# Two more buffers for streamed expert weights, and a small product moved from the first eight experts to the last eight

## The reference

```python
a = rms_norm(h, g_mix)
o, sg, sh = parallel_mixers(a, ...)                # one input and one output projection
h = h + o
h = h + moe(rms_norm(h, g_ffn), w_router, b_router, w_gu, b_gu, w_dn, b_dn)
gate = sigmoid(rms_norm(h, g_ple) @ w_ple_gate)
h = h + gate * (p @ w_ple_proj)                    # p: 256 input-embedding features a token
y = rms_norm(h, g_final)
```

```python
gate, up = split(x @ w_gu[e] + b_gu[e], 2)         # w_gu[e]: 1024 x 2048
hid = (clip(up) + 1) * (min(gate, 7) * sigmoid(1.702 * gate))
y = hid @ w_dn[e] + b_dn[e]                        # w_dn[e]: 1024 x 1024
```

## Time and profile before

| | |
|---|---|
| median of 3 runs | 1286.03 us |
| profiled execution | 1286.39 us |
| its span, first to last instruction | 1284.2 us |
| TensorE busy in the span | 1216.6 us |
| bytes moved by DMA | 437.59 MB, 402.65 MB of them expert weights (384 units of 1 MB) |
| expert stage | from about 260 us to about 1231 us of the span |

### The profile page before, as it was taken

How to read it: one execution, slowest core, us unless ns; L and a number is a source line. 1 busy time by engine, 2 the same in 40 slices (tenths; PEclk the granted TensorE clock), 3 DMA queues, 4 the chain that set the end, 5 groups by cost and what they waited for, 6 DMA issues and landing times.

```text
span 1284.2 us, 12672 instructions
## 1 busy us (share of the span) xinstructions
PE 1216.6 (95%) x5435; PEld 582.6 (45%) x5436; DVE 271.1 (21%) x493; ACT 192.0 (15%) x316; POOL 33.9 (3%) x47
## 2 busy tenths in 40 slices
PE   7999999999999999999999999999999999988896
PEld 4778767653444444444443333333333333323265
DVE  1246634211111111111211111111111111111123
ACT  2141122311111111010111101110101010101033
POOL 3002020000000000000000000000000000000000
PEclk9999977989999999999999999999999999999999
DMA  7462622969999999999999999999999999999920
GB/s 178 113 164 66 160 82 72 389 229 380 418 418 401 419 415 417 417 417 417 416 418 417 417 417 417 417 418 417 417 418 416 418 416 417 417 417 417 415 101 37
DMA packets 127359, 437.59 MB, mean 341 GB/s; under 512 B 9580, under 2 KB 59848, under 8 KB 94504
## 3 DMA queue, kind: packets, MB, share of 16 engines
q1 hardware_dynamic: 123872, 433.75, 85.3%
q10 hardware_dynamic: 3256, 2.78, 0.7%
q0 software_dynamic: 176, 0.27, 0.1%
HBM read 432.04 MB, written 4.72 MB: 340 GB/s over the span
## 4 chain that ended last, share of the span: by engine, by line
PE 52%; DMA 39%; SPq 4%; DVE 2%; ACT 1%; ACTq 1%; issue 1%; DVEq 0%
PE ps L774 50%; DMA ring<-in_w_gu 38%; SPq L474 4%; DMA ring<-in_w_ple_gate 1%; PE ps L1101 0%; ACTq L586 0%; DVE ring L1304 0%; PE ps L1123 0%; ACT tok L691 0%; ACTq L581 0%; PE ps L851 0%; ACT L602 0%; PE ps L842 0%; DVE ring L1385 0%; DVE ring L1314 0%
## 5 line engine op out<-in xcount | busy, mean ns | idle before, releaser
L774 PE MATMUL ps<-ring,s 128*64 128x512 f32 x1024 | 231.5, 596 | 18.9 <-DMA ring<-in_w_gu 18.7
L774 PE MATMUL ps<-ring,aT 128*64 128x512 f32 x1024 | 228.8, 595 | 11.5 <-DMA ring<-in_w_gu 11.4
L774 PE MATMUL ps<-ring,wst 128*64 128x512 f32 x1024 | 232.1, 598 | 2.7 <-ACT wst L719 2.7
L1530 DVE TENSOR_SCALAR wst<-ps 128x512 f32<-128x512 f32 x32 | 22.1, 692 | 751.6 <-PE ps L774 751.6
L774 PEld LDWEIGHTS ps<-ring,s 128*64 128x64 f32 x1024 | 69.8, 137 | 177.9 <-issue 118.5
L774 PEld LDWEIGHTS ps<-ring,aT 128*64 128x64 f32 x1024 | 70.9, 137 | 165.5 <-issue 127.4
L774 PEld LDWEIGHTS ps<-ring,wst 128*64 128x64 f32 x1024 | 68.6, 136 | 130.9 <-issue 126.6
L774 PE MATMUL ps<-aT,wst 128*128 128x288 f32 x384 | 100.3, 423 | 3.0 <-ACT ring L625 3.0
L717 ACT ACTIVATE wst<-wst 128x512 f32<-128x512 f32 x32 | 20.2, 630 | 516.0 <-DVE wst L1530 516.0
L774 PE MATMUL ps<-sel,tok 128*128 128x256 f32 x384 | 96.1, 390 | 1.0 <-DVE sel L1492 1.0
L774 PEld LDWEIGHTS ps<-aT,wst 128*128 128x128 f32 x384 | 75.3, 198 | 28.5 <-issue 4.2
(11 more groups left out here) (233 smaller groups left out, 681.5 us busy)
## 6 DMA issues: line engine op xcount, KB each, us to landing
ring<-in_w_gu SPq DMA_DIRECT2D x256, 1024.0 KB, 19.8
ring<-in_w_dn SPq DMA_DIRECT2D x128, 1024.0 KB, 23.5
wst<-in_w_in SPq DMA_DIRECT2D x28, 512.0 KB, 3.8
wst<-in_w_out SPq DMA_DIRECT2D x8, 512.0 KB, 3.7
ring<-in_w_ple_gate SPq DMA_DIRECT2D x4, 1024.0 KB, 16.7
ring<-in_state_hgrn SPq DMA_DIRECT2D x4, 512.0 KB, 6.2
out<-ring SPq DMA_DIRECT2D x4, 512.0 KB, 4.2
tok<-in_x_prompt ACTq DMA_DIRECT2D x1, 1024.0 KB, 6.5
```

The source lines that it names most:

```text
L774: return pe.matmul(o, lhsT, rhs, start=start, stop=stop, skip_group_check=True)
L1530: dve.tensor_scalar(gbuf, ps[:, 0, :], SWIGLU_LIMIT, None, ALU.min).then_inc(gate_ready, 1)
```

## The change

The stream gets 14 places instead of 12: `vmask` and the first 2048 columns of `acc`. To free `vmask`, `b_dn` and `gateT` go to rows 32 to 63 of `bgu` (whose rows 0 to 31 hold `b_gu`), and `lgs` goes to `lnbuf`. Places are dealt in the order in which they come free, not by the unit's number. `acc` leaves the deal before unit 264 (= 22 x 12), since from expert 24 on the small product is written there: it now stands in experts 24 to 31. The load of `b_dn` moves to the front of SP's program, behind a wait for the load of `b_gu`. The four places for `w_ple_gate` are the four that come free first.

```diff
+        lgs = lnbuf[0:E, :]
+        b_dn = bgu[E:2 * E, 0:D]
+        gateT = bgu[E:2 * E, D:D + T]
...
+        slots = [ring[:, c * UCOLS:(c + 1) * UCOLS] for c in range(UNITS)]
+        slots.append(vmask[:].rearrange("p i b v -> p (i b v)"))
+        slots.append(acc[:].rearrange("p c t -> p (c t)")[:, 0:UCOLS])
+        V_SLOT, A_SLOT = UNITS, UNITS + 1
+        PP0 = E - KD
+        slot_of, before, turn = [], [], []
+        queue = [(i, None) for i in range(UNITS + 2)]
+        for u in range(U_ALL):
+            i, prev = queue.pop(0)
+            if i == A_SLOT and u >= (PP0 - 2) * UNITS:
+                i, prev = queue.pop(0)
+            turn.append(slot_of.count(i) + 1)
+            slot_of.append(i)
+            before.append(prev)
+            queue.append((i, u))
+        last_use = {i: u for u, i in enumerate(slot_of)}
+        pg_slots = sorted((i for i in range(UNITS)), key=lambda i: last_use[i])[0:KD // 2]
...
             for i in range(LATE + G):
                 load_cols(i)
+                if i == G:
+                    sp.wait_ge(bgu_loaded, 16)
+                    sp.dma_start(b_dn, io["b_dn"][0]).then_inc(bdn_loaded, 16)
...
-            for e in range(1, E):
-                for c in range(UNITS):
-                    sp.wait_ge(u_used, (e - 1) * UNITS + c + 1)
-                    sp.dma_start(unit_dst(c), unit_src(e, c)).then_inc(u_loaded[c], 16)
+            for u in range(UNITS, U_ALL):
+                e, c = u // UNITS, u % UNITS
+                if u == A_SLOT:
+                    sp.wait_ge(h_done, KD)
+                if before[u] is not None:
+                    sp.wait_ge(u_used, before[u] + 1)
+                sp.dma_start(as_unit(weights(e, c), c), unit_src(e, c)).then_inc(u_loaded[slot_of[u]], 16)
...
             for c in range(KD // 2):
-                sp.wait_ge(u_used, U_ALL - UNITS + c + 1)
+                sp.wait_ge(u_used, last_use[pg_slots[c]] + 1)
...
-                    if c == 2 and e < KD:
-                        if e:
-                            pe.wait_ge(pp_copied, e)
+                    if c == 2 and e >= PP0:
+                        i = e - PP0
+                        if i == 0:
+                            pe.wait_ge(u_used, last_use[A_SLOT] + 1)
                         for k in range(PLE // P):
-                            ins = mm(ps[:, 4, 0:T], w_pp[:, k, e * P:(e + 1) * P], pT[:, k, :], k == 0, k == PLE // P - 1)
+                            ins = mm(ps[:, 4, 0:T], w_pp[:, k, i * P:(i + 1) * P], pT[:, k, :], k == 0, k == PLE // P - 1)
                         ins.then_inc(pp_done, 1)
```

More of the change, by code:

```diff
@@ L171, in build @@
         vmask = sb("vmask", [P, 2, SB, P])
-        after_v = vmask[:, 1].rearrange("e b v -> e (b v)")
-        lgs = after_v[0:E, 0:T]
-        gateT = after_v[:, T:2 * T]
         rcol = sb("rcol", [P, NT])
@@ L183, in build @@
         maski = sb("maski", [P, P + 32], I32)
-        b_dn = vmask[:, 0].rearrange("e b v -> e (b v)")
         seqmask = sb("seqmask", [32, SB])
@@ L316, in build @@
         cnt_ready = sem("cnt_ready")
-        u_loaded = [sem(f"u_loaded{i}") for i in range(UNITS)]
+        u_loaded = [sem(f"u_loaded{i}") for i in range(UNITS + 2)]
         u_used = sem("u_used")
@@ L382, in unit_src, with weights, wait_weights, as_unit @@
             return io["w_dn"][0, e, c * P:(c + 2) * P, :].rearrange("(c p) n -> p c n", p=P)
+        slots = [ring[:, c * UCOLS:(c + 1) * UCOLS] for c in range(UNITS)]
[14 more added lines that the diff above has]
+        last_use = {i: u for u, i in enumerate(slot_of)}
+        assert last_use[A_SLOT] < PP0 * UNITS
+        pg_slots = sorted((i for i in range(UNITS)), key=lambda i: last_use[i])[0:KD // 2]
+        def weights(e, c):
+            return slots[slot_of[e * UNITS + c]]
+        def wait_weights(eng, e, c):
+            u = e * UNITS + c
+            eng.wait_ge(u_loaded[slot_of[u]], 16 * turn[u])
+        def as_unit(v, c):
+            return v if c < KD else v.rearrange("p (c n) -> p c n", c=2)
         def unit_dst(c):
-            v = ring[:, c * UCOLS:(c + 1) * UCOLS]
-            return v if c < KD else v.rearrange("p (c n) -> p c n", c=2)
+            return as_unit(slots[c], c)
         def most_rows(eng):
@@ L461, in _ @@
             sp.wait_ge(su_done, HEADS)
-            sp.dma_start(b_dn[0:E, :], io["b_dn"][0]).then_inc(bdn_loaded, 16)
             sp.wait_ge(o_ready, HEADS)
@@ L468, in _ @@
                     load_cols(NZ + WSLOTS + c)
-                sp.dma_start(unit_dst(c), unit_src(0, c)).then_inc(u_loaded[c], 16)
-            for e in range(1, E):
-                for c in range(UNITS):
-                    sp.wait_ge(u_used, (e - 1) * UNITS + c + 1)
-                    sp.dma_start(unit_dst(c), unit_src(e, c)).then_inc(u_loaded[c], 16)
+                sp.dma_start(unit_dst(c), unit_src(0, c)).then_inc(u_loaded[slot_of[c]], 16)
+            for u in range(UNITS, U_ALL):
[5 more added lines that the diff above has]
+                sp.dma_start(as_unit(weights(e, c), c), unit_src(e, c)).then_inc(u_loaded[slot_of[u]], 16)
             most = most_rows(sp)
@@ L490, in _ @@
             for c in range(KD // 2):
-                sp.wait_ge(u_used, U_ALL - UNITS + c + 1)
-                sp.dma_start(ring[:, c * UCOLS:(c + 1) * UCOLS].rearrange("p (c n) -> p c n", c=2),
+                sp.wait_ge(u_used, last_use[pg_slots[c]] + 1)
+                sp.dma_start(slots[pg_slots[c]].rearrange("p (c n) -> p c n", c=2),
                              io["w_ple_gate"][0, 2 * c * P:(2 * c + 2) * P, :].rearrange("(c p) n -> p c n", p=P)) \
@@ L695, in _ @@
             act.wait_ge(gateT_done, 1)
-            act.copy(gateT[0:E, :], ps[0:E, 0, 0:T]).then_inc(gateT_copied, 1)
+            act.copy(gateT, ps[0:E, 0, 0:T]).then_inc(gateT_copied, 1)
             def copy_gathered(g, j):
@@ L724, in _ @@
                     act.copy(selT[:], ps[:, 3, 0:T]).then_inc(st_copied, 1)
-                if e < KD:
-                    act.wait_ge(pp_done, e + 1)
-                    act.copy(acc[:, e, :], ps[:, 4, 0:T]).then_inc(pp_copied, 1)
+                if e >= PP0:
+                    act.wait_ge(pp_done, e - PP0 + 1)
+                    act.copy(acc[:, e - PP0, :], ps[:, 4, 0:T]).then_inc(pp_copied, 1)
             copy_rows(E - 1)
@@ L1071, in gate_up @@
             def gate_up(e, c):
-                pe.wait_ge(u_loaded[c], 16 * e + 16)
+                wait_weights(pe, e, c)
                 if e % QUAD == 0 and c % 2 == 0:
@@ L1076, in gate_up @@
                 for b in range(2):
-                    w0 = c * UCOLS + b * FF
-                    ins = halves(b, xsT[e // QUAD % 2][:, c, e % QUAD, :], ring[:, w0:w0 + BANK], ring[:, w0 + BANK:w0 + FF],
+                    w, w0 = weights(e, c), b * FF
+                    ins = halves(b, xsT[e // QUAD % 2][:, c, e % QUAD, :], w[:, w0:w0 + BANK], w[:, w0 + BANK:w0 + FF],
                                  False, c == KD - 1)
@@ L1111, in _ @@
                 for c in range(KF // 2):
-                    pe.wait_ge(u_loaded[KD + c], 16 * e + 16)
+                    wait_weights(pe, e, KD + c)
                     for k in range(2):
@@ L1115, in _ @@
                         x0 = (kc % (KF // 2)) * P + (kc // (KF // 2)) * SLOTS
-                        w0 = (KD + c) * UCOLS + k * D
-                        ins = halves(5, hidT[:, x0:x0 + SLOTS], ring[:, w0:w0 + BANK], ring[:, w0 + BANK:w0 + D],
+                        w, w0 = weights(e, KD + c), k * D
+                        ins = halves(5, hidT[:, x0:x0 + SLOTS], w[:, w0:w0 + BANK], w[:, w0 + BANK:w0 + D],
                                      kc == 0, kc == KF - 1)
@@ L1125, in _ @@
                         ins.then_inc(st_done, 1)
-                    if c == 2 and e < KD:
-                        if e:
-                            pe.wait_ge(pp_copied, e)
+                    if c == 2 and e >= PP0:
+                        i = e - PP0
+                        if i == 0:
+                            pe.wait_ge(u_used, last_use[A_SLOT] + 1)
                         for k in range(PLE // P):
-                            ins = mm(ps[:, 4, 0:T], w_pp[:, k, e * P:(e + 1) * P], pT[:, k, :], k == 0, k == PLE // P - 1)
+                            ins = mm(ps[:, 4, 0:T], w_pp[:, k, i * P:(i + 1) * P], pT[:, k, :], k == 0, k == PLE // P - 1)
                         ins.then_inc(pp_done, 1)
-                if e < KD:
-                    pe.wait_ge(pp_copied, e + 1)
+                if e >= PP0:
+                    pe.wait_ge(pp_copied, e - PP0 + 1)
             most = most_rows(pe)
@@ L1152, in extra_block @@
                     x0 = (c % (KD // 2)) * P + (c // (KD // 2)) * SLOTS
-                    pe.wait_ge(u_loaded[c], n * 16 + (16 * E + 16))
+                    pe.wait_ge(u_loaded[c], n * 16 + 16 * (turn[last_use[c]] + 1))
                     for b in range(2):
@@ L1167, in extra_block @@
                 for c in range(KF // 2):
```

(4 more changed lines are left out.)

## The result

The changed kernel took 1281.33 us (median of 14 runs, 1273.79 to 1283.27), the kernel before 1287.32 us beside it (median of 14, 1280.77 to 1288.98). The ratio is 0.9945, with an interval of 0.9929 to 0.9962: 7.1 us less, between 4.9 and 9.1; the two medians alone lie 6.0 us apart, which is inside that interval. The forecast was 5.7 us less. The profiled execution took 1280.12 us, with a span of 1277.9 us against 1284.2 us.

What follows compares the result with a forecast made beforehand. The prediction took the expert stage's stream of weight loads, 2.51 us a unit plus its standing time, as the bound. Terms -5.0 - 1.0 + 0 + 0.3 = -5.7 us gave 1280.3 us against the 1286.03 us median; range 1278.0 to 1283.2 us.

Steps and rivals of the forecast that it cites:

- What bounds the kernel: Expert stage: a stream of 384 loads at 2.51 us each; only the time in which it stands still can change.
- Two more places: Hole at 262 to 274 us: units 12 and 13 load early and fill 5.0 of 11.4 us; -5.0 us.
- The small product leaves experts 0 to 7: PE frees units 1.17 us sooner per expert passed, closing holes behind removed chunks; -1.0 us, bounds 0 and 2.4 us.
- the earlier hole: Stretch between 300 and 310 us where the stream stood for 1.1 us, behind the chunk of expert 0.
- the later hole: Stretch between 385 and 405 us where the stream stood for 1.3 us, behind four chunks; busy DMA share 1.01.
- `b_dn` with 32 rows: Experts 2 and 3: 16 row-count changes at 0 to 0.14 us, covered by PE's 4.7 us gain; 0 us.
- the bound without cover: If PE's 4.7 us gain and the places failed to cover `b_dn`'s row changes, at most 1.3 us would stay.
- The small product in experts 24 to 31: Beside PE's waiting in seven experts, on PE's path only in expert 31; +0.3 us, bounds 0 and +1.2 us.
- The wait for `w_ple_gate`: Behind the last combine PE waited 0.91 us for these weights; this wait should be gone.
- The signs: Expected in the profile: shorter hole at 262 us, chain period 30.1 us, earlier but less waiting, last `w_gu` 5 to 7 us sooner.
- the rate at 300 to 310 us: Sign: the DMA rate in this window should be near 418 GB/s.
- The rival in which all holes close: All holes behind a removed chunk close: -5.0 - 2.4 + 0.3 = -7.1 us, 1278.9 us; chance 0.13.

Runs made afterwards that it cites:

- e2: The changed kernel with 12 places, no added place; small product in experts 24 to 31, `b_dn` alternating: ratio 0.9983 to the kernel before, stage 958.7 us.
- e9: The changed kernel (14 places) with the products of `b_dn` in experts 2 and 3 grouped instead of alternating: ratio 0.9942 to the kernel before, stage 953.9 us.
- e7: e1 with the products of `b_dn` in experts 2 and 3 grouped instead of alternating: ratio 1.0011 to the kernel before, stage 960.1 us.
- e1: Kernel before plus only the moves of `b_dn`, `gateT`, `lgs`, early `b_dn` load and `w_ple_gate` order; 12 places, product in experts 0 to 7: ratio 1.0022.
- e3: The changed kernel with 13 places: `vmask` dealt, `acc` not: ratio 0.9969 to the kernel before, stage 955.3 us.
- e6: The changed kernel with 15 places and the small product in experts 23 to 30: ratio 0.9941 to the kernel before, stage 951.0 us.
- e4: The changed kernel with a fifteenth place laid over small tiles dead after the ranks are counted: ratio 0.9921 to the kernel before, stage 950.6 us.
- e8: The changed kernel with 15 places, `b_dn` products grouped, small product in experts 23 to 30: ratio 0.9928 to the kernel before, stage 950.3 us.

## Why the prediction was right

- *What bounds the kernel.* Right. The steady rate stayed at 417 GB/s in all of these kernels, and each place brought the stream's end about one unit nearer (2.6 to 2.9 us).
- *Two more places, -5.0 us.* Right: 5.3 us of stage from e2 to the changed kernel, 5.5 us up to the last unit of `w_gu`. The issue of unit 12 was not done right after the loads ahead of it, as I had put it, but took 11 us, without harm. The wait for `h_done` held nothing; the second load was issued at 249.83 us.
- *The small product leaves experts 0 to 7, -1.0 us.* Right in kind, short in size, wrong in place. I expected the earlier hole to close; 0.8 us of its 1.1 us stayed, and the later one (1.3 us) closed. That is 1.6 us, and e2, which has no added place, ends its stream 1.7 us sooner than before. The reason given for taking less than 2.4 us, the busy share of 1.01 in the later hole, did not decide: that hole closed in full.
- *`b_dn` with 32 rows, 0 us.* Right for this kernel, because the product's move covers it: e9 gains nothing by grouping. The price of a change was set at 0.14 us and measured 0.2 us. That 32 rows might be faster, which gave the lower bound of the price, is not borne out (e7). Wrong was the bound without cover, 1.3 us: I had taken the hole of before as the most that could remain, but a hole grows when PE gets later, and e1 shows about 3 us. The two edits are not independent terms: without the product's move these moves cost 3 us, and with them in place the product's move is worth 4.
- *The small product in experts 24 to 31, +0.3 us.* The mechanism held in seven of the eight experts, where PE waits for the stream, but the end lost 1.1 us. The wait for `w_ple_gate`, which should have gone, stayed. It is the last load of `w_ple_gate`: it came 21.3 us after the last unit of `w_gu` instead of 20.2 us, and PE still waited 0.69 us for it. Why that load was 1.1 us later is not settled. Most of it needs neither the late product nor a place: in e1 and e7, which have neither, the end takes 20.8 and 21.0 us. In e3 the end went as forecast: no wait, and 20.6 us where 20.5 had been worked out, so there the product in the last expert was on PE's path; in e6 it was not.
- *The signs.* The period of the chain stayed, PE was not idle at the late chunks, and it waited less for weights there (9.0 us between 955 and 1203 us, where it had waited 14.0 us between 966 and 1209 us) and began to wait earlier (at 657 instead of 666 us). Two signs failed: the rate at 300 to 310 us, and the wait for `w_ple_gate`. The last unit of `w_gu` came 7.4 us sooner, a little outside the 5 to 7 us.
- *The whole.* 5.7 us forecast, 7.1 us measured (4.9 to 9.1), 6.1 us in the stage of the two profiles. The profiles make this 1.7 us from the holes, 5.5 us from the places and 1.1 us lost at the end, against 1.0, 5.0 and 0.3: the first two were too small by 1.2 us, the last by 0.8 us. That the sum came so near is in part luck. The rival in which all holes close had 7.1 us too; the ratio cannot choose between it and the forecast, but the windows show that 1.6 of its 2.4 us closed, and its term for the end was 0.8 us too small.

## What to carry to other kernels

Where a stream of loads runs at one rate whatever its depth (here 417 GB/s with 12 to 15 places), its end is moved only by the time in which it stands still: find those stretches in a table of windows, and price a buffer by what fits into them, here 2.6 to 2.9 us for each of the first three. With the third the hole was not yet full, so where the gain stops was not seen. Work on another engine counts only where the stream waits for it, so the price of an edit there depends on what else is changed: test it with and without its cover. A busy engine (95% here) says little if it still waits a fraction of a microsecond at every unit.

## What was not expected of the hardware

Single executions of one kernel differ by up to 10 us, and the profiles show where: before the expert stage, in TensorE's granted clock. These are the windows from 60 to 235 us, first of e6, then of the changed kernel, then of e4:

```profile
60.00:235.00 175.00, 171.84 (x731) 125.87 (x729) 84.67 (x137) 44.47 (x63) 19.69 (x10) 0.89 0.42 116
```

```profile
60.00:235.00 175.00, 171.85 (x745) 125.94 (x744) 85.45 (x139) 44.91 (x64) 19.68 (x10) 0.91 0.44 124
```

```profile
60.00:235.00 175.00, 171.84 (x767) 126.40 (x766) 86.25 (x141) 45.42 (x65) 19.69 (x10) 0.94 0.47 135
```

The mean granted clock is 0.89, 0.91 and 0.94 of full speed, a mixture of 1.2 and 2.4 GHz, and PE is busy for the same 171.8 us. SP's first issue released by PE then comes at 274.80, 272.05 and 266.41 us. All ten profiles fall into this order: e1 with 0.90 has it at 274.21 us; before, e3, e7 and e9 with 0.91 at 271.9 to 272.3 us; e2 with 0.93 at 269.31 us; e8 with 0.94 at 266.62 us. The expert stage behind hardly shows it: with 15 places it takes 950.6 and 950.3 us in e4 and e8, and 951.0 us in e6. What makes the clock differ between executions was not tried.

The other is the thirteenth load of 1 MB, whose issue was held on SP for 10.97 us, although nothing in the program waits there. All six kernels with more than 12 places show it, with 10.41 to 10.97 us. What sets that time was not tried.
